# A hybrid decoder block with a routed expert layer: the steps between the output projection and the expert loop re-ordered in quarters and halves

## The reference, cut to what matters

```python
x = x + mix @ w_o
h2 = rms_norm(x, g_ffn)
logits = h2 @ w_router + b_router          # 32 experts
top_val, top_idx = lax.top_k(logits, 4)
top_w = softmax(top_val)
# for every expert e, over the tokens xb that chose it:
hid = xb @ w_up[e] + b_up[e]               # 1024 -> 2048
glu, lin = hid[..., ::2], hid[..., 1::2]
glu, lin = min(glu, 7), clip(lin, -7, 7)
ys = (glu * sigmoid(1.702 * glu) * (lin + 1)) @ w_down[e] + b_down[e]   # 1024 -> 1024
x = x + sum of ys * top_w over the four experts of a token
```

## Time and profile before

| | |
|---|---|
| median of the three runs | 1306.62 us (1305.88 to 1310.32) |
| profiled execution, its own time | 1308.24 us |
| its span in the profile | 1306.3 us |
| TensorE busy | 1247.7 us, 96% |
| VectorE busy | 367.7 us, 28% |
| ScalarE busy | 283.4 us, 22% |
| bytes moved by DMA | 452.58 MB, mean 346 GB/s |

### The profile page before, as it was taken

One profiled execution on the slowest core, in us unless ns is written; L12 is line 12 of the kernel. 1 busy time (PEld: TensorE's weight loads), 2 busy tenths in 40 slices (PEclk: granted clock), 3 DMA queues, 4 the chain that ended last, 5 costly groups with the idle time before them and its releaser, 6 DMA issues.

```text
span 1306.3 us, 14461 instructions
## 1 busy us (share of the span) xinstructions
PE 1247.7 (96%) x5617; PEld 545.5 (42%) x5617; DVE 367.7 (28%) x1016; ACT 283.4 (22%) x559; POOL 47.6 (4%) x102
## 2 busy tenths in 40 slices
PE   9999999999999999999999999989999998999997
PEld 7887456644453333333333333333333333333332
DVE  4576825664332112211121111211111111221111
ACT  3231122243122121211221112211111121121112
POOL 3040110110000000000000000000000000000000
PEclk9999999999999999999999999999999999999999
DMA  7772533374748999999999999999999999999996
GB/s 234 138 230 74 200 99 111 104 282 160 303 186 359 428 429 427 428 426 428 427 428 427 428 427 428 427 428 428 426 428 428 428 428 426 427 428 428 428 426 259
DMA packets 57770, 452.58 MB, mean 346 GB/s; under 512 B 10760, under 2 KB 10904, under 8 KB 33136
## 3 DMA queue, kind: packets, MB, share of 16 engines
q1 hardware_dynamic: 53552, 447.24, 82.8%
q0 software_dynamic: 1568, 3.72, 1.7%
q10 hardware_dynamic: 2592, 0.79, 0.3%
HBM read 448.17 MB, written 3.15 MB: 345 GB/s over the span
## 4 chain that ended last, share of the span: by engine, by line
PE 59%; DMA 33%; DVE 4%; ACT 2%; issue 1%; SPq 0%; ACTq 0%; PEldq 0%
DMA ring<-in_w_up_dram 26%; PE pb L1472 19%; PE pb L1509 11%; PE pb L1205 9%; PE pb L1186 4%; DMA last_slot<-in_w_up_dram 4%; PE pb L1435 4%; DMA ring<-in_w_in_dram 3%; PE pb L1423 2%; PE pb L1351 2%; PE pb L1172 2%; DVE ring L910 1%; DVE ring L909 1%; PE pb L1429 1%; PE pb L1494 1%
## 5 line engine op out<-in xcount | busy, mean ns | idle before, releaser
L1472 PE MATMUL pb<-ring,buf_a 128*64 128x512 f32 x1856 | 418.2, 595 | 26.8 <-DMA ring<-in_w_up_dram 26.8
L1472 PEld LDWEIGHTS pb<-ring,buf_a 128*64 128x64 f32 x1856 | 128.4, 136 | 276.2 <-issue 218.2
L1131 DVE TENSOR_SCALAR buf_a<-pb 128x256 f32<-128x256 f32 x64 | 26.9, 421 | 722.9 <-PE pb L1472 722.9
L1509 PE MATMUL pb<-ring,buf_b 128*64 128x512 f32 x944 | 209.7, 595 | 7.7 <-ACT buf_b L756 6.9
L1205 PE MATMUL pb<-ring,last_slot 128*128 128x512 f32 x384 | 173.3, 597 | 0.9 <-PE pb L1205 0.6
L1509 PEld LDWEIGHTS pb<-ring,buf_b 128*64 128x64 f32 x944 | 65.4, 137 | 131.4 <-issue 116.3
L735 ACT ACT_TABLE_LOAD x32 | 41.1, 1283 | 304.9 <-PE pb L1423 304.9
L1205 PEld LDWEIGHTS pb<-ring,last_slot 128*128 128x128 f32 x384 | 69.8, 190 | 78.4 <-issue 77.4
L1186 PE MATMUL pb<-last_slot,ring 128*128 128x256 f32 x384 | 89.7, 388 | 1.1 <-DMA ring<-in_w_in_dram 1.1
L1186 PEld LDWEIGHTS pb<-last_slot,ring 128*128 128x128 f32 x384 | 72.7, 193 | 11.1 <-issue 1.4
L758 ACT COPY buf_b<-pb 128x512 f32<-128x512 f32 x32 | 18.7, 585 | 222.7 <-PE pb L1509 222.7
(11 more groups left out here) (286 smaller groups left out, 875.5 us busy)
## 6 DMA issues: line engine op xcount, KB each, us to landing
ring<-in_w_up_dram SPq DMA_DIRECT2D x116, 2048.0 KB, 43.2
ring<-in_w_down_dram SPq DMA_DIRECT2D x59, 2048.0 KB, 46.7
ring<-in_w_in_dram SPq DMA_DIRECT2D x18, 2048.0 KB, 8.3
last_slot<-in_w_up_dram SPq DMA_DIRECT2D x12, 2048.0 KB, 47.0
last_slot<-in_w_down_dram SPq DMA_DIRECT2D x5, 2048.0 KB, 35.8
ring<-in_w_o_dram SPq DMA_DIRECT2D x2, 2048.0 KB, 14.2
t_rows<-ring POOLq DMA_DIRECT2D x1, 1536.0 KB, 34.8
xt<-in_x_dram SPq DMA_DIRECT2D x2, 512.0 KB, 4.2
```

The source lines that it names most:

```text
L1131: v.tensor_scalar(glu[:, cols], pairs[:, :, 0], LIMIT, None, ALU.min).then_inc(s_glu, 1)
L1472: ins = mm(pb[64 * hf:64 * hf + 64, n_, :], xg[:, c, :], slot(s)[:, at_:at_ + 512], start=False, stop=(c == KC - 1), skip_group_check=True)
L1509: ins = mm(pb[64 * hf:64 * hf + 64, 2, :], actT[:, j, hf_in, :], slot(s)[:, at_:at_ + 512], start=(c == 0), stop=(c == KC - 1), skip_group ...
```

## The change

Ahead of the loop, the last half of the residual, its transposes and its copies are done in two quarters each; ScalarE takes the square root directly from its own sums of squares, and VectorE takes the reciprocal afterwards; the indices are compared without the cast to float; `select` signals after each token block and `gather` waits for each block by itself; the first copy of the gathered rows is made in halves, and the `awake` matmuls are 2 in place of 4, and none in place of 3.

In the loop and ahead of it, `turn_rows(rows, i)` writes its two halves to columns 256 to 511 of banks 2 and 3, where before all went to bank 3; `take_gathered(i)` takes each half by itself; the bias products no longer wait for `xg`, the up projection does, at chunk 0 and at chunk 2. Since bank 2 is shared with the gate transposes and with the down result, `turn_rows` in the loop also waits for the copy of the down result of the expert before, and the gate transposes wait for the first half of `take_gathered`.

```diff
-                act_e.wait_ge(s_x1, 2 * b + n_ + 1)
+                if b and n_:
+                    act_e.wait_ge(s_x1q, 2)
+                else:
+                    act_e.wait_ge(s_x1, 2 * b + n_ + 1)
...
+            def root_of_squares(b):
+
+                act_e.wait_ge(s_var, ROOTS.index(f"r{b}") + 1)
+                act_e.wait_ge(s_sst, 2 * b + 2)
+                sc.activation(rt2[:, b:b + 1], ssp[:, b, 1:2], ACT.Sqrt, bias=ss[:, b:b + 1], scale=1.0 / D).then_inc(s_root, 1)
...
             act_e.wait_ge(s_gath, 1)
-            sc.copy(sgm, pb[:, 3, :]).then_inc(s_xgt, 1)
+            for i in range(2):
+                sc.copy(sgm[:, 256 * i:256 * i + 256], pb[:, 3, 256 * i:256 * i + 256]).then_inc(s_xgt, 1)
...
-                link(v.tensor_scalar(x_, ssp[:, b, 0:1], 1.0 / D, EPS, ALU.mult, ALU.add))
-                link(v.scalar_tensor_tensor(out=x_, in0=ssp[:, b, 1:2], scalar=1.0 / D, in1=x_, op0=ALU.mult, op1=ALU.add))
-                v.reciprocal(w_, x_).then_inc(s_var, 1)
+                link(v.scalar_tensor_tensor(out=lg[:, b, 0:1], in0=ssp[:, b, 1:2], scalar=1.0 / D, in1=x_, op0=ALU.mult, op1=ALU.add))
                 dve.wait_ge(s_root, ROOTS.index(f"r{b}") + 1)
+                link(v.reciprocal(y, w_))
...
-                link(v.tensor_copy(idxf[:, b, :], idx_u[:, b, :]))
...
+            def first_square_mean(b):
+
+                dve.wait_ge(s_sst, 2 * b + 1)
+                v.tensor_scalar(ss[:, b:b + 1], ssp[:, b, 0:1], 1.0 / D, EPS, ALU.mult, ALU.add).then_inc(s_var, 1)
+                dve.wait_ge(s_var, ROOTS.index(f"r{b}") + 1)
...
-            residual(1, 1)
-            dve.wait_ge(s_xtr1, 4)
-            v.tensor_copy(x1T[:, 4:8, P:T], pb[:, 1, :].rearrange("p (c t) -> p c t", c=4)).then_inc(s_xTl, 1)
+            first_square_mean(1)
+            dve.wait_ge(s_wo, 4)
+            for i in range(2):
+                cols = slice(512 + 256 * i, 768 + 256 * i)
+                v.tensor_tensor(xt[:, 1, cols], xt[:, 1, cols], pb[:, 5, 256 * i:256 * i + 256], ALU.add).then_inc(s_x1q, 1)
+            for i in range(2):
+                dve.wait_ge(s_xtrq, i + 1)
+                v.tensor_copy(x1T[:, 4 + 2 * i:6 + 2 * i, P:T], pb[:, 1 - i, 0:256].rearrange("p (c t) -> p c t", c=2)).then_inc(s_xTl, 1)
...
-                    ins = v.tensor_scalar(sel[:, b, :], iota_s[:, 0:SLOTS], posm[:, b, col], rr[:, b:b + 1], ALU.is_equal, ALU.mult)
-                ins.then_inc(s_sel, 1)
+                    v.tensor_scalar(sel[:, b, :], iota_s[:, 0:SLOTS], posm[:, b, col], rr[:, b:b + 1], ALU.is_equal, ALU.mult).then_inc(s_sel, 1)
...
+            for s_ in (s_glu, s_lin, s_actT):
+                dve.sem_inc(s_, 2)
+            for i in range(2):
+                dve.wait_ge(s_xtr, i + 1)
+                take_gathered(i)
...
                     v.tensor_copy(selE[:, :], seleye[:, bass.ds(k + 1, 1)].to_broadcast([96, SLOTS])).then_inc(s_sele, 1)
-                    dve.wait_ge(s_xtr, k + 2)
-                    take_gathered()
+                    for i in range(2):
+                        dve.wait_ge(s_xtr, 2 * k + i + 3)
+                        take_gathered(i)
...
-            turn(1, 1)
-            awake(4)
+            for i in range(2):
+                pe.wait_ge(s_x1T, 2 + i)
+                pe.wait_ge(s_x1q, i + 1)
+                for c in range(2):
+                    ins = nc.tensor.transpose(pb[:, 1 - i, c * P:(c + 1) * P], xt[:, 1, 512 + (2 * i + c) * P:512 + (2 * i + c + 1) * P], ident)
+                ins.then_inc(s_xtrq, 1)
+            awake(2)
...
-            pe.wait_ge(s_sel, 1)
-            gather()
+            gather(0)
+            for i in range(2):
+                pe.wait_ge(s_xgt, i + 1)
+                turn_rows(sgm, i)
             open_sum(1, 1)
-            pe.wait_ge(s_xgt, 1)
-            turn_rows(sgm)
             pe.wait_ge(s_gpad, 1)
+            pe.wait_ge(s_xg, 1)
...
-            awake(3, 1)
...
-                    pe.wait_ge(s_xg, k + 1)
                     pe.wait_ge(s_actT, 2 * k + 2)
...
                     for c, n_ in UP_ORDER:
+                        if c in (0, 2) and n_ == 0:
+                            pe.wait_ge(s_xg, 2 * k + c // 2 + 1)
...
                         elif (c, n_) == (5, 1):
-                            pe.wait_ge(s_xgt, k + 2)
-                            turn_rows(xgt)
+                            pe.wait_ge(s_xgt, k + 3)
+                            pe.wait_ge(s_ys, k + 1)
+                            for i in range(2):
+                                turn_rows(xgt, i)
 
                     pe.wait_ge(s_ys, k + 1)
                     pe.wait_ge(s_selg, k + 1)
+                    pe.wait_ge(s_xg, 2 * k + 3)
                     for b in range(NB):
                         ins = nc.tensor.transpose(pb[:, 2, b * P:(b + 1) * P], selg[:, b, :], ident)
```

More of the change, by code:

```diff
@@ L313, in block_kernel @@
         s_ml, s_bdn, s_wrt = sem("moe_params_loaded"), sem("b_down_loaded"), sem("router_scaled")
-        s_xtr1, s_x1T, s_xTl, s_zero, s_gpad = sem("x1_transposed"), sem("x1T_ready"), sem("last_x1T_ready"), sem("moe_tiles_zeroed"), sem("padded_gates_ready")
+        s_xtr1, s_x1T, s_xTl, s_zero, s_gpad = sem("x1_transposed"), sem("x1T_ready"), sem("last_x1T_quarters_ready"), sem("moe_tiles_zeroed"), sem("padded_gates_ready")
         s_sst = sem("x1_half_squares")
+        s_x1q, s_xtrq = sem("last_x1_quarters_ready"), sem("last_x1_quarters_transposed")
         s_slab = [sem(f"slab_loaded_{i}") for i in range(NSLOT)]
@@ L319, in block_kernel @@
         s_gath, s_xgt, s_xtr = sem("tokens_gathered"), sem("gathered_rows_taken"), sem("gathered_transposed")
-        s_xg, s_up0, s_up, s_glu, s_lin = sem("tokens_ready"), sem("up_first_half_done"), sem("up_done"), sem("glu_ready"), sem("lin_ready")
+        s_xg, s_up0, s_up, s_glu, s_lin = sem("token_halves_ready"), sem("up_first_half_done"), sem("up_done"), sem("glu_ready"), sem("lin_ready")
         s_sgm, s_actv, s_actr, s_actT = sem("swiglu_sigmoid_done"), sem("act_ready"), sem("act_transposed"), sem("actT_ready")
@@ L719, in _ @@
             half_squares(0, 1)
-            root("r0", rr[:, 0:1], rt2[:, 0:1])
+            root_of_squares(0)
             take_turned(0, 1)
@@ L724, in _ @@
             half_squares(1, 1)
-            root("r1", rr[:, 1:2], rt2[:, 1:2])
+            root_of_squares(1)
             for b in range(NB):
@@ L733, in take_rows @@
                 act_e.wait_ge(s_gath, k + 1)
-                act_e.wait_ge(s_xtr, k)
+                act_e.wait_ge(s_xtr, 2 * k)
                 sc.copy(xgt, pb[:, 3, :]).then_inc(s_xgt, 1)
             act_e.wait_ge(s_gath, 1)
-            sc.copy(sgm, pb[:, 3, :]).then_inc(s_xgt, 1)
+            for i in range(2):
+                sc.copy(sgm[:, 256 * i:256 * i + 256], pb[:, 3, 256 * i:256 * i + 256]).then_inc(s_xgt, 1)
             act_e.wait_ge(s_gtt, 1)
@@ L1030, in inverse_rms @@
                 dve.wait_ge(s_sst, 2 * b + 2)
-                link(v.tensor_scalar(x_, ssp[:, b, 0:1], 1.0 / D, EPS, ALU.mult, ALU.add))
-                link(v.scalar_tensor_tensor(out=x_, in0=ssp[:, b, 1:2], scalar=1.0 / D, in1=x_, op0=ALU.mult, op1=ALU.add))
-                v.reciprocal(w_, x_).then_inc(s_var, 1)
+                link(v.scalar_tensor_tensor(out=lg[:, b, 0:1], in0=ssp[:, b, 1:2], scalar=1.0 / D, in1=x_, op0=ALU.mult, op1=ALU.add))
                 dve.wait_ge(s_root, ROOTS.index(f"r{b}") + 1)
-                link(v.scalar_tensor_tensor(out=w_, in0=y, scalar=x_, in1=y, op0=ALU.mult, op1=ALU.mult))
+                link(v.reciprocal(y, w_))
+                link(v.scalar_tensor_tensor(out=w_, in0=y, scalar=lg[:, b, 0:1], in1=y, op0=ALU.mult, op1=ALU.mult))
                 link(v.tensor_scalar(w_, w_, -0.5, 1.5, ALU.mult, ALU.add))
                 link(v.tensor_tensor(y, y, w_, ALU.mult))
+            def first_square_mean(b):
+                dve.wait_ge(s_sst, 2 * b + 1)
+                v.tensor_scalar(ss[:, b:b + 1], ssp[:, b, 0:1], 1.0 / D, EPS, ALU.mult, ALU.add).then_inc(s_var, 1)
+                dve.wait_ge(s_var, ROOTS.index(f"r{b}") + 1)
             def choose(b):
@@ L1044, in choose @@
                 link(v.max_index(idx_u[:, b, :], top8[:, b, :], lg[:, b, :]))
-                link(v.tensor_copy(idxf[:, b, :], idx_u[:, b, :]))
-                link(v.tensor_tensor(oh4[:, b], iota_e[:, None, :].to_broadcast([P, TOP_K, E]), idxf[:, b, 0:TOP_K, None].to_broadcast([P, TOP_K, E]), ALU.is_equal))
+                link(v.tensor_tensor(oh4[:, b], iota_e[:, None, :].to_broadcast([P, TOP_K, E]), idx_u[:, b, 0:TOP_K, None].to_broadcast([P, TOP_K, E]), ALU.is_equal))
                 v.tensor_reduce(chob[:, b, :], oh4[:, b].rearrange("p j e -> p e j"), AX_X, ALU.max).then_inc(s_cho, 1)
@@ L1062, in _ @@
             v.tensor_tensor(wrt[:, :, :], wrt[:, :, :], gffn_c[:, :, None].to_broadcast([P, KC, E]), ALU.mult).then_inc(s_wrt, 1)
+            first_square_mean(0)
             inverse_rms(0)
```

(35 more changed lines are left out.)

1 line of the change is left out of this document (removed).

## The result

The changed kernel takes 1393.1 us in the median of four runs (1389.99 to 1400.1), 1.0658 times the time of before, with a 95% interval of 1.0632 to 1.0684. That is 86 us slower, where 47 had been forecast: the direction and the place were right, the size was not, and the range that ended at 1366 does not hold the time.

The account below looks back on a forecast made before the run. Transfers bound the loop's later part at 29.37 us an expert; the change makes TensorE bind at 29.71. 32 x (2.71 - 1.21) = 48.0, less 0.9, gives +47.1 on 1306.62: 1353.7 us, range 1344 to 1366.

Parts of the forecast that it names:

- The free 1.21 us: Expert loop: TensorE may be 1.21 us slower per expert without harm; each further us costs 32.
- The wait behind VectorE's whole activation chain: Gate transposes in the loop: waiting for `take_gathered`'s first half starts them 2.71 us later per expert, costing 48.0 us.
- Nothing behind it absorbs a part: Combine, turned activations, down projection and next expert, behind the gate transposes: all move by the full 2.71 us.
- The start of the loop: Steps ahead of the expert loop: the edits start the loop 0.9 us earlier, ends 0.5 and 1.4.
- The clock falls: Rival, in the loop: TensorE's clock halves for combine and transposes, 64 us more, 1418 us; chance 0.04.
- More is lost than the pause: Rival, in the loop: restart or bunched transfers cost extra; at 0.6 us an expert, 1373 us; chance 0.06.

Follow-up runs that it names:

- wait_sigmoid: The kernel before, with the gate transposes made to wait for ScalarE's second sigmoid; ratio 1.002.
- combine_first: The changed kernel with the combine moved ahead of the added wait and the gate transposes in the loop; 1311.91 us, ratio 1.0025.
- filled_pause: The changed kernel with 16 unused matmuls of 256 columns put into TensorE's pause, the work behind starting no earlier; 1353.57 us, ratio 1.0342.
- half_filled: The changed kernel with 8 unused matmuls of 256 columns in TensorE's pause; 1359.71 us, ratio 1.0403.
- wait_product: The kernel before, with the gate transposes made to wait for VectorE's second product; ratio 1.0106.
- early_take: The whole changed kernel with the first half of `take_gathered` moved ahead of the clamps in VectorE's loop; 1307.75 us, ratio 0.9994.

## Why the prediction was right and wrong

- **The free 1.21 us and 32 us for each further one: right within 4 us.** It holds over delays from 1.17 to 2.60 us where the clock stays up. Below the bound it is a little too kind: wait_sigmoid and combine_first should cost nothing and cost about 3 us.
- **The wait behind VectorE's whole activation chain: right**, in place, cause and nearly in size. The delay was 2.59 by the pace, not 2.71: the first half of `take_gathered` lets TensorE go 0.47 after its start where I had added 0.42 and 0.21. The term was 44.1 us, not 48.0. The kernel with only this term, filled_pause, measures 1353.6; the forecast was 1353.7. That they agree to 0.1 is partly luck, since the kernel before measured 1308.4 beside filled_pause and 1306.6 when the forecast was made; as a cost it is 45 against 47.
- **Nothing behind it absorbs a part: right**; the down projection moves with the gate transposes. Where only those two transposes wait and the combine does not (combine_first), the loss is nearly gone.
- **The start of the loop: 0.68 us earlier, 0.9 forecast**; too small to be measured in the time.
- **The failed step: the sum had no term for the clock.** It took TensorE to stay at 1.00 behind a new pause of 2.6 us in each expert, and set the fall apart as the second rival, "The clock falls", with a chance of 0.04 and outside the range. The runs showed 37.1 us for it in the place of nothing, which is what takes the time out of the range.
- **The ground for the 0.04 did not carry.** It was that the clock stays at 1.00 over pauses of 1.24 us and that TensorE is evenly busy around a single pause. 1.24 was also misread as the longest: the transfer-bound part of the kernel before has one pause of 1.80 us, with the clock at 1.00.

```profile
1094.43 3.65 PE L1472 MATMUL pb<-ring,buf_a 128*64 128x512 f32 x16 [1.80 <-DMA ring<-in_w_up_dram]
```

  Neither pause says anything of one of 2.6 us in every expert. No row of the loop showed one, so neither outcome was ruled out, and the fall should have been in the range.
- **The rival's working did not hold either**: it let the clock fall in each of the 32 experts, at 2 us each. It fell in 23 of them and cost about 1.6 us each time, mostly in the combine, and so 37 us and not 64. The Trainium skill ("TensorE: Matmul & The Clock Gate", HAM oscillation) says that idle gaps that come in each turn of a loop can halve the array's clock each time. The trace agrees in kind, with 0.57 granted behind a pause of 2.49 us. It differs in two ways, and there the measurement decides: the page has this for longer gaps than the one here, and has every turn hit, where here 9 of 32 are spared.
- **"More is lost than the pause" was not it**: in filled_pause nothing is lost beyond the delay, with the same restart of what follows.

What stays open is which pauses the clock forgives. Equal pauses of 2.49 us are followed by a fall in 23 of 32 cases and by none in 9, and a pause of 1.5 us in 6 of 32 in half_filled, but none of 1.6 us in the loop of wait_product.

## What to carry to other kernels

A wait on another engine costs what stands ahead of the awaited instruction in that engine's list, not what the instruction itself takes: here 0.4 us of work stood behind 2 us of activation, and moving it into idle time cured all of it (early_take, 0.9994). Work out first how much delay an engine beside the bounding one can take (here 38.8 us over 32 turns); below that a new wait is free, above it the cost is multiplied by the turns. And price a new idle stretch of TensorE twice, once for its length and once for the clock behind it, above all when it is longer than any that the trace shows at full clock. A shorter one is not safe either when it comes in every turn: half_filled lost the clock 6 times behind 1.5 us, while the single pause of 1.80 us in the kernel before kept it.

## What the runs showed of the hardware that I had not expected

A pause of 2.49 us in 31 of otherwise busy TensorE time lowered the granted clock behind it in 23 of 32 experts, and 16 matmuls of no use in that pause, which left 0.6 us of it, took 40 us off the time. Which experts are spared follows a pattern: in the changed kernel every third or fourth of the distances is an undisturbed 29.6, and in half_filled the falls come in pairs about 358 us apart (at 502 and 533, 861 and 891, 1219 and 1250 us). The pauses of one kernel are equal, so their length alone does not decide. The pattern would fit that it also matters when a pause comes, but no run varies that alone, so this is not shown.
